# Neighbourhood attention on one core: the maxima of the next two heads taken ahead of this two's weights on VectorE

## The chip, the cores and the metric

The kernel runs on one core of one Trainium2 chip. The metric is the time of one execution on the device in microseconds (us), a median of several runs. All times below are us unless marked ns. TensorE is called PE in the profile's rows, VectorE DVE, ScalarE ACT, GpSimd POOL, SyncE SP; PEld is TensorE's weight load.

## What is computed

The whole program is two blocks of a model one after the other, with a batch of one: a first block (two layers of feed-forward, a pool/convolution/retention mixer, feed-forward) and a second block of an even layer (neighbourhood attention beside an mLSTM) and an odd layer (latent attention). The change lies in the neighbourhood attention of the even layer, over 8 heads of 64 features, 256 context tokens and 256 latent tokens (4 rows of 64). Cut to what matters:

```python
s_lat = einsum('bqhd,bkhd->bhqk', q_row, k_band) * scale + bias   # latent keys, learned bias and window
s_ctx = einsum('bqhd,bkhd->bhqk', q_row, k_c) * scale             # 256 context keys
p = softmax(concatenate([s_lat, s_ctx], axis=-1), axis=-1)
out = einsum('bhqk,bkhd->bqhd', p[..., :nl], v_band) + einsum('bhqk,bkhd->bqhd', p[..., nl:], v_c)
na_c = dense_attention(heads(naq_c), heads(nak_c), heads(nav_c))  # context tokens over context keys
```

## The kernel before

Each engine has an order of instructions written out by hand, and the engines are tied by counting semaphores alone. An engine takes its instructions in that order; `wait_ge(s, n)` stops everything behind it on its engine until semaphore `s` has reached `n`.

The attention of the even layer is cut into 16 pairs, `EVEN_PAIRS`. A pair is 128 queries of two heads (`e` is 0 or 1, the first and the second head of the pair). Pairs 0 to 7 are context queries over 256 keys; pairs 8 to 15 are latent queries over 512 keys, whose bias is added by a further product on TensorE. For each pair `p` the steps are:

- scores on TensorE (`scores(p)`): two products, for pairs 8 to 15 followed by the bias product of either head. Each head has a PSUM bank; there are four banks (2, 3, 0, 1), so that the scores of pair `p + 1` take the banks of pair `p - 1`, and wait until its weights are made (`at_exp`).
- maximum on VectorE (`top(p)`, L2599 and L2600): for each head a `tensor_reduce` of the scores into a column of the small tile `STAT`, then a `tensor_scalar` that makes the negative bias of it. Both wait for the scores (`at_scores`), and signal `at_max`.
- weights on ScalarE (`weights(p)`, L1868): `exp` of the scores into `probs[e]` (tile `PR`), with the sum of each row. It waits for `at_max`, and for the turning of pair `p - 1`, since `PR` has one buffer for each head.
- normalisation on VectorE (`norm(p)`, L2606 and L2608): reciprocal of the sum, and `PR` times it. It waits for `at_exp` and signals `at_probs`.
- turning on TensorE (`turn(p)`, L1202): transposes of `PR` into PSUM, which wait for `at_probs`; ScalarE copies them (`copy_turned`, L1878, tile `PTT`).
- values on TensorE (`values(p)`), the copy of the result by ScalarE (`place_high`, L1884) and the low part of it by VectorE (`place`, L2614).

TensorE's order around pair `p` is scores(p + 1), turn(p), values(p - 1), and then at some pairs a product of the mLSTM's head norm (`between`, `head_norm`): a mean, a variance or a spread, over 512 columns. VectorE's part of the head norm is L2581 (subtract the mean), L2585 and L2590, ScalarE's L1848, L1851, L1854 and L1858. The engines that follow wait for the last pair: `even_output` on TensorE begins with `pe.wait_ge(at_out, len(EVEN_PAIRS))`.

The same function `attend` serves the odd layer's latent attention (`base` is then 16 and not 0), with its tiles `PRO` and `PTO`.

Of the kernel before, what the change touches and what calls it, by code (L numbers as in the profile page):

```python
# [11 lines left out]
ALU = mybir.AluOpType  # L12
ACT = mybir.ActivationFunctionType
AX = mybir.AxisListType
# [57 lines left out]
def build(nc, A, out):  # L72
    with ExitStack() as ctx:
        def sem(name):
            return ctx.enter_context(nc.semaphore(name))
# [102 lines left out]
        STAT = low.put("STAT", [64])  # L178
# [86 lines left out]
        def values_of(b):  # L265

            return PS[:, 6, 0:P] if b < len(EVEN_PAIRS) else PS[:, 6 + b % 2, 0:P]
# [85 lines left out]
        def halves(name):  # L353
# [11 lines left out]
        at_scores, at_max, at_exp, at_probs, at_turned, at_copied, at_pv, at_high, at_out = (  # L365
            sem("at_scores"), sem("at_max"), sem("at_exp"), sem("at_probs"), sem("at_turned"), sem("at_copied"),
            sem("at_pv"), sem("at_high"), sem("at_out"))
# [1074 lines left out]
        def _(act):  # L1442
# [417 lines left out]
            def softmax(pairs, base, probs, turned, banks, between):  # L1860
                def weights(p):
                    w = pairs[p]["keys"]
                    for e in range(2):
                        n = 2 * (base + p) + e
                        act.wait_ge(at_max, n + 1)
                        if p >= 1:
                            act.wait_ge(at_turned, n - 1)
                        act.activation(probs[e][:, 0:w], PS[:, banks[(2 * p + e) % len(banks)], 0:w], ACT.Exp,  # L1868
                                       bias=STAT[:, 4 + e:5 + e], scale=pairs[p]["scale"],
                                       accum_out=STAT[:, 8 + e:9 + e]).then_inc(at_exp, 1)  # L1870

                def copy_turned(p):
                    nk = pairs[p]["keys"] // P
                    for e in range(2):
                        act.wait_ge(at_turned, 2 * (base + p) + e + 1)
                        if base + p >= 1:
                            act.wait_ge(at_pv, base + p)
                        act.copy(turned[e][:, 0:nk, :], PS[:, 4 + e, 0:nk * P].rearrange("p (a b) -> p a b", a=nk))\  # L1878
                            .then_inc(at_copied, 1)

                def place_high(p):
                    b = base + p
                    act.wait_ge(at_pv, b + 1)
                    act.copy(pairs[p]["out"][0], values_of(b)).then_inc(at_high, 1)  # L1884

                for p in range(len(pairs)):
                    weights(p)
                    if p >= 2 and base == 0:
                        place_high(p - 2)
                    if p >= 1:  # L1890
                        copy_turned(p - 1)
                    if p >= 2 and base:
                        place_high(p - 2)
                    between(2 * p)
                    between(2 * p + 1)
                copy_turned(len(pairs) - 1)
                place_high(len(pairs) - 2)
                place_high(len(pairs) - 1)
# [133 lines left out]
        def _(v):  # L2032
# [342 lines left out]
            vs = Steps(v, vec_step)  # L2375
# [216 lines left out]

            def attend(pairs, base, probs, banks, between):
                def top(p):
                    w = pairs[p]["keys"]
                    for e in range(2):
                        v.wait_ge(at_scores, 2 * (base + p) + e + 1)
                        src = PS[:, banks[(2 * p + e) % len(banks)], 0:w]
                        vs.link(v.tensor_reduce(STAT[:, e:e + 1], src, AX.X, ALU.max))  # L2599
                        v.tensor_scalar(STAT[:, 4 + e:5 + e], STAT[:, e:e + 1], -pairs[p]["scale"], None, ALU.mult)\  # L2600
                            .then_inc(at_max, 1)

                def norm(p):
                    for e in range(2):
                        v.wait_ge(at_exp, 2 * (base + p) + e + 1)
                        vs.link(v.reciprocal(STAT[:, 12 + e:13 + e], STAT[:, 8 + e:9 + e]))  # L2606
                        q = probs[e][:, 0:pairs[p]["keys"]]
                        v.tensor_scalar(q, q, STAT[:, 12 + e:13 + e], None, ALU.mult).then_inc(at_probs, 1)  # L2608

                def place(p):  # L2610
                    b = base + p
                    v.wait_ge(at_high, b + 1)
                    hi, lo = pairs[p]["out"]
                    v.tensor_tensor(lo, values_of(b), hi.bitcast(F32), ALU.subtract).then_inc(at_out, 1)  # L2614

                top(0)
                for p in range(len(pairs)):
                    norm(p)
                    if p >= 2 and base == 0:
                        place(p - 2)  # L2620
                    if p + 1 < len(pairs):
                        top(p + 1)
                    if p >= 2 and base:
                        place(p - 2)
                    between(2 * p)
                    between(2 * p + 1)
                for p in range(len(pairs) - 2, len(pairs)):
                    place(p)
# [110 lines left out]
            even_inputs()  # L2739
            mlstm()  # L2740
            attend(EVEN_PAIRS, 0, PR, (2, 3, 0, 1), lambda n: head_norm(n - HEAD_SHIFT))
            even_output()
            ffn_both()
            odd_inputs()
            attend(ODD_PAIRS, len(EVEN_PAIRS), PR2, (0, 1, 2, 3), lambda n: None)
            rest(O_WO + 3)
            odd_output()
# [182 lines left out]
```

## Time and profile before

| | us |
|---|---|
| median of 3 runs | 2183.38 (2182.88 to 2185.84) |
| the profiled execution | 2183.48 |
| its span in the trace | 2181.6 |
| TensorE busy in the span | 2115.5 (97%) |
| VectorE busy | 1570.3 (72%) |
| ScalarE busy | 1054.4 (48%) |

The profiled execution is within 0.1 us of the median, and 1.9 us of it lie outside of the span. The attention of the even layer runs from 1300.34, where TensorE begins the scores of pair 0, to 1374.88, where it begins the output product: 74.5 us. That of the odd layer runs from 1869.84 to some 1935. Times of single rows are from the start of the span. Where the trace gives the records of a group of matmuls, their duration reaches from the first start to the last end, which is modelled.

### The profile page before, as it was taken

Reading aid. Unit: us, or ns where it says so; the run is one execution under the profiler, and the core shown is the slowest. Engines: PE = TensorE matmul, PEld = TensorE weight load, DVE = VectorE, ACT = ScalarE, POOL = GpSimd, SP = SyncE. Lnnn points to the kernel's source line nnn. Section 1 sums busy time; section 2 is a strip of 40 time slices with the busy share of each in tenths; the row PEclk is TensorE's granted clock in tenths of the full one; section 3 lists DMA queues with packets and bytes.
Section 4 is the critical chain, followed back from the end, with each engine's and each line's share of the span. In section 5 each row is a group of like instructions: output and inputs, shape, how many; then the busy total and the mean of one; then the engine's idle time right before and its main releaser. Section 6 shows DMA issues by size and latency. Waiting matters only on the chain. (4 is left out here: it accounts for less than half of the span.)

```text
span 2181.6 us, 35138 instructions
## 1 busy us (share of the span) xinstructions
PE 2115.5 (97%) x14758; PEld 1927.2 (88%) x14758; DVE 1570.3 (72%) x2371; ACT 1054.4 (48%) x1546; POOL 156.4 (7%) x195
## 2 busy tenths in 40 slices
PE   8999999999999999999999988999999999999997
PEld 8999989999999998999897775898888887579997
DVE  6878998877988798988852667466555346858774
ACT  6443656443544465644552446345444224746652
POOL 1200102201200100200100000000000001000000
PEclk9999999999999999999999999999999999999998
DMA  7665526666566543777331120123222222023552
GB/s 272 234 232 203 206 97 251 234 241 250 208 233 245 206 155 116 272 273 257 125 120 54 59 97 13 55 78 115 97 97 97 97 89 82 24 78 118 191 175 97
DMA packets 48334, 334.93 MB, mean 154 GB/s; under 512 B 5612, under 2 KB 6716, under 8 KB 8880
## 3 DMA queue, kind: packets, MB, share of 16 engines
q1 hardware_dynamic: 38384, 267.47, 34.6%
q0 software_dynamic: 9792, 65.21, 7.8%
q8 instruction: 117, 1.92, 0.4%
q14 instruction: 41, 0.34, 0.0%
HBM read 331.61 MB, written 1.05 MB: 152 GB/s over the span
## 5 line engine op out<-in xcount | busy, mean ns | idle before, releaser
L2042 DVE TENSOR_TENSOR WLO<-RAW,WHI 128x2048 fp32r<-128x2048 f32 x252 | 574.7, 2285 | 217.9 <-ACT WHI L1457 215.2
L464 PE MATMUL PS<-XB,WHI 128*128 128x256 f32 (+1 forms) x3072 | 697.4, 322 | 8.3 <-DVE XB L2398 4.0
L1457 ACT CAST WHI<-RAW 128x2048 fp32r<-128x2048 f32 x252 | 476.6, 1894 | 281.0 <-DMA RAW<-in_dn_c 78.4
L464 PEld LDWEIGHTS PS<-XB,WHI 128*128 128x128 f32 x3072 | 513.9, 191 | 55.7 <-issue 11.0
L464 PE MATMUL PS<-XHI,WHI 128*128 128x272 f32 (+1 forms) x1760 | 498.4, 290 | 5.8 <-ACT XHI L1465 5.8
L464 PE MATMUL PS<-XB,WLO 128*128 128x256 f32 (+1 forms) x1536 | 492.1, 320 | 0.0
L464 PE MATMUL PS<-XHI,WLO 128*128 128x272 f32 (+1 forms) x1760 | 489.7, 288 | 0.0
L464 PE MATMUL PS<-XLO,WHI 128*128 128x272 f32 (+1 forms) x1760 | 482.1, 287 | 2.3 <-DVE XLO L2088 2.3
L464 PEld LDWEIGHTS PS<-XHI,WHI 128*128 128x128 f32 x1760 | 328.8, 189 | 9.8 <-issue 8.8
L464 PEld LDWEIGHTS PS<-XLO,WHI 128*128 128x128 f32 x1760 | 323.0, 189 | 4.1 <-DVE XLO L2088 3.6
L464 PEld LDWEIGHTS PS<-XHI,WLO 128*128 128x128 f32 x1760 | 326.0, 188 | 0.0
L464 PEld LDWEIGHTS PS<-XB,WLO 128*128 128x128 f32 x1536 | 292.8, 191 | 21.3
L464 PE MATMUL PS<-GHI,WHI 128*128 128x272 f32 (+1 forms) x704 | 200.1, 286 | 0.0
L464 PE MATMUL PS<-GHI,WLO 128*128 128x272 f32 (+1 forms) x704 | 199.7, 285 | 0.0
L464 PE MATMUL PS<-GLO,WHI 128*128 128x272 f32 (+1 forms) x672 | 191.9, 286 | 0.0
L2442 DVE SCALAR_TENSOR_TENSOR AC<-CB,FCW,AC 128x512 f32<-128x512 f32 (+1 forms) x176 | 97.1, 614 | 131.6 <-ACT AC L1715 103.8
L464 PEld LDWEIGHTS PS<-GHI,WLO 128*128 128x128 f32 x704 | 132.5, 188 | 0.0
L464 PEld LDWEIGHTS PS<-GHI,WHI 128*128 128x128 f32 x704 | 132.4, 188 | 0.0
L1517 ACT ACTIVATE SG<-PS 128x272 f32<-128x272 f32 (+1 forms) x88 | 34.5, 393 | 201.1 <-PE PS L464 200.7
L2071 DVE CUSTOM_DVE_ANT_0 PROD<-AW,SCB,ADAB 128x1024 f32<-128x1024 f32 x96 | 130.9, 1364 | 0.3 <-ACT SCB L1445 0.3
L2071 DVE CUSTOM_DVE_ANT_0 AW<-AW,SCB,ADAB 128x1024 f32<-128x1024 f32 x96 | 127.0, 1323 | 0.0
L464 PEld LDWEIGHTS PS<-GLO,WHI 128*128 128x128 f32 x672 | 126.4, 188 | 0.0
(364 smaller groups left out, 2517.0 us busy)
## 6 DMA issues: line engine op xcount, KB each, us to landing
AW<-in_ada POOLq DMA_DIRECT2D x48, 1024.0 KB, 7.1
RAW<-in_up_c SPq DMA_DIRECT2D x44, 1024.0 KB, 4.9
RAW<-in_up_a SPq DMA_DIRECT2D x42, 1024.0 KB, 5.2
RAW<-in_up_b SPq DMA_DIRECT2D x42, 1024.0 KB, 4.9
RAW<-in_mix SPq DMA_DIRECT2D x30, 1024.0 KB, 4.9
RAW<-in_dn_a SPq DMA_DIRECT2D x22, 1024.0 KB, 4.9
RAW<-in_dn_b SPq DMA_DIRECT2D x22, 1024.0 KB, 5.0
RAW<-in_dn_c SPq DMA_DIRECT2D x22, 1024.0 KB, 5.0
```

The costliest lines, as they stand in the source:

```text
L464: return pe.matmul(o, w, x, start=first, stop=last)
L1457: act.copy(WHI1[:, s, 0:w], RAW[:, s, 0:w]).then_inc(w1_high, 1)
L1517: act.activation(SG[r, f % 2, tk], PS[r, 2 * (f % 3), tk], ACT.Silu).then_inc(silu1_done, 1)
L2042: v.tensor_tensor(WLO1[:, s, 0:w], RAW[:, s, 0:w], WHI1[:, s, 0:w].bitcast(F32), ALU.subtract)\
L2071: v.tensor_tensor_reduce(PROD[:, :] if g == 0 else w, w, SCB[:, g, :], 1.0, ADAB[:, t:t + 1], ALU.mult, ALU.add, MODF[:, t, g:g + 1]).then ...
L2442: return v.scalar_tensor_tensor(o, i, vec(a, t), o, ALU.mult, ALU.add)
```

## The change

In `attend`, VectorE takes `top(p + 1)` ahead of `norm(p)` for the even layer, where it took it behind `norm(p)` and `place(p - 2)`. For the odd layer (`base` not 0) the order stays. As the maxima of pair `p + 1` are now written while the sums of pair `p` are still to be used, the columns of `STAT` come in two sets, 16 columns apart, chosen by `p % 2`, on VectorE and on ScalarE, in both layers.

```diff
@@ ScalarE, weights(p)
                         act.activation(probs[e][:, 0:w], PS[:, banks[(2 * p + e) % len(banks)], 0:w], ACT.Exp,
-                                       bias=STAT[:, 4 + e:5 + e], scale=pairs[p]["scale"],
-                                       accum_out=STAT[:, 8 + e:9 + e]).then_inc(at_exp, 1)
+                                       bias=STAT[:, 16 * (p % 2) + 4 + e:16 * (p % 2) + 5 + e], scale=pairs[p]["scale"],
+                                       accum_out=STAT[:, 16 * (p % 2) + 8 + e:16 * (p % 2) + 9 + e]).then_inc(at_exp, 1)
@@ VectorE, attend
                 def top(p):
-                    w = pairs[p]["keys"]
+                    w, c = pairs[p]["keys"], 16 * (p % 2)
...
-                        vs.link(v.tensor_reduce(STAT[:, e:e + 1], src, AX.X, ALU.max))
+                        vs.link(v.tensor_reduce(STAT[:, c + e:c + e + 1], src, AX.X, ALU.max))
...
                 def norm(p):
                     for e in range(2):
                         v.wait_ge(at_exp, 2 * (base + p) + e + 1)
-                        vs.link(v.reciprocal(STAT[:, 12 + e:13 + e], STAT[:, 8 + e:9 + e]))
+                        c = 16 * (p % 2) + e
+                        vs.link(v.reciprocal(STAT[:, c + 12:c + 13], STAT[:, c + 8:c + 9]))
...
                 top(0)
                 for p in range(len(pairs)):
+                    if p + 1 < len(pairs) and base == 0:
+                        top(p + 1)
                     norm(p)
                     if p >= 2 and base == 0:
                         place(p - 2)
-                    if p + 1 < len(pairs):
+                    if p + 1 < len(pairs) and base:
                         top(p + 1)
```

How VectorE's instructions stand in a row where the latent queries are worked on. PR_138 and PR_139 are the weights of the first and second head of the pair; the words in brackets are the semaphores. Before, between the placing of pair 6 and that of pair 7:

```order
L2606 RECIPROCAL STAT<-STAT 128x1 [waits at_exp]
L2608 TENSOR_SCALAR PR_138<-PR_138,STAT 128x512 [waits vec_step]
L2606 RECIPROCAL STAT<-STAT 128x1 [waits at_exp]
L2608 TENSOR_SCALAR PR_139<-PR_139,STAT 128x512 [waits vec_step]
L2614 TENSOR_TENSOR XB<-PS,XB 128x128 [waits at_high]
L2599 TENSOR_REDUCE STAT<-PS 128x1 [waits at_scores]
L2600 TENSOR_SCALAR STAT<-STAT 128x1 [waits vec_step]
L2599 TENSOR_REDUCE STAT<-PS 128x1 [waits at_scores]
L2600 TENSOR_SCALAR STAT<-STAT 128x1 [waits vec_step]
```

With the change:

```order
L2599 TENSOR_REDUCE STAT<-PS 128x1 [waits at_scores]
L2600 TENSOR_SCALAR STAT<-STAT 128x1 [waits vec_step]
L2599 TENSOR_REDUCE STAT<-PS 128x1 [waits at_scores]
L2600 TENSOR_SCALAR STAT<-STAT 128x1 [waits vec_step]
L2607 RECIPROCAL STAT<-STAT 128x1 [waits at_exp]
L2609 TENSOR_SCALAR PR_138<-PR_138,STAT 128x512 [waits vec_step]
L2607 RECIPROCAL STAT<-STAT 128x1 [waits at_exp]
L2609 TENSOR_SCALAR PR_139<-PR_139,STAT 128x512 [waits vec_step]
L2615 TENSOR_TENSOR XB<-PS,XB 128x128 [waits at_high]
```

The two maxima of the next pair, with their wait for its scores, now stand ahead of the normalisation of this pair and of the placing. The lines of the functions below `top` are one higher in the changed kernel.

TensorE's row is the same in both kernels. For the latent queries, from the scores of pair `p + 1` on (G and BIAS are operands of the scores and the bias, IDN of the turning, PTT of the values):

```order
L464 MATMUL PS<-G 128x512 [waits at_exp,at_max]
L464 MATMUL PS<-G 128x512
L464 MATMUL PS<-BIAS_146,IDN_115 128x256 [waits tab_loaded]
L464 MATMUL PS<-BIAS_146,IDN_115 128x256
L1202 MATMUL PS<-IDN,PR_138 128x128 [waits at_copied,at_probs]
L1202 MATMUL PS<-IDN,PR_138 128x128 x3
L1202 MATMUL PS<-IDN,PR_139 128x128 [waits at_copied,at_probs]
L1202 MATMUL PS<-IDN,PR_139 128x128 x3
L464 MATMUL PS<-PTT_140,VN 64x128 [waits at_out,at_copied]
```

Nothing moved here: the turning of pair `p` (L1202) stands directly behind the scores and the bias of pair `p + 1`.

## Rows read from the trace of the kernel before

**Rows 1.** The page's first part: busy time of each engine

```profile
PE 2115.5 (97%) x14758; PEld 1927.2 (88%) x14758; DVE 1570.3 (72%) x2371; ACT 1054.4 (48%) x1546; POOL 156.4 (7%) x195
```

**Rows 2.** Stretches: length, busy time (instructions) of each engine, PE clock, DMA

```profile
1300.34:1326.50 26.16, 20.35 (x121) 9.86 (x120) 18.83 (x70) 13.74 (x49) 2.65 (x5) 0.93 0.28 101
1326.50:1369.00 42.50, 36.98 (x256) 22.79 (x255) 29.86 (x85) 28.66 (x72) 0.00 (x0) 0.98 0.08 26
1869.80:1935.00 65.20, 61.63 (x449) 39.28 (x449) 50.91 (x145) 44.96 (x114) 0.04 (x1) 1.00 0.03 12
```

**Rows 3.** Waits, 1300.3 to 1374.9: waiter, waited for, total, times, longest

```profile
ACT PR L1868 <- DVE STAT L2600: 9.1, 9, 2.6
PE PS L1202 <- DVE PR L2608: 7.6, 6, 2.8
...
PE PS L1202 <- ACT PTT L1878: 3.6, 3, 2.1
```

**Rows 4.** Timeline at pair 14, 512 keys: start, duration, instructions [idle before]

```profile
1362.71 0.69 DVE L2599 TENSOR_REDUCE STAT<-PS 128x1 f32<-128x512 f32 x1 [1.05 <-PE PS L464]
...
1362.94 1.04 PE L1202 MATMUL PS<-IDN,PR 128*128 128x128 f32 x8
...
1364.29 0.74 DVE L2585 SCALAR_TENSOR_TENSOR G<-G,MLG,PS 128x512 f32<-128x512 f32 x1
```

**Rows 5.** Timeline, VectorE: one normalisation over 512 keys

```profile
1336.21 0.16 DVE L2606 RECIPROCAL STAT<-STAT 128x1 f32<-128x1 f32 x1 [2.28 <-ACT PR L1868]
...
1336.41 0.49 DVE L2608 TENSOR_SCALAR PR<-PR,STAT 128x512 f32<-128x512 f32 x1
```

**Rows 6.** Timeline at pair 6, 256 keys

```profile
1324.30 0.65 PE L1202 MATMUL PS<-IDN,PR 128*128 128x128 f32 x4
...
1324.40 0.42 DVE L2599 TENSOR_REDUCE STAT<-PS 128x1 f32<-128x256 f32 x1 [0.18 <-PE PS L464]
...
1325.45 0.68 DVE L2581 TENSOR_TENSOR G<-G,PS 128x512 f32<-128x512 f32 x1
```

**Rows 7.** Timeline at pair 2: normalisation, and the turning that waits for it

```profile
1310.13 0.35 DVE L2608 TENSOR_SCALAR PR<-PR,STAT 128x256 f32<-128x256 f32 x1
...
1310.54 0.90 PE L1202 MATMUL PS<-IDN,PR 128*128 128x128 f32 x4 [0.58 <-DVE PR L2608]
```

**Rows 8.** Timeline: the turnings of pairs 0, 4, 7, 9, 12 and 15

```profile
1303.01 0.90 PE L1202 MATMUL PS<-IDN,PR 128*128 128x128 f32 x4 [1.53 <-DVE PR L2608]
...
1317.62 0.68 PE L1202 MATMUL PS<-IDN,PR 128*128 128x128 f32 x4 [2.10 <-ACT PTT L1878]
...
1328.27 0.68 PE L1202 MATMUL PS<-IDN,PR 128*128 128x128 f32 x4 [0.61 <-ACT PTT L1878]
...
1337.63 1.12 PE L1202 MATMUL PS<-IDN,PR 128*128 128x128 f32 x8 [1.40 <-DVE PR L2608]
...
1352.72 1.11 PE L1202 MATMUL PS<-IDN,PR 128*128 128x128 f32 x8 [0.69 <-DVE PR L2608]
...
1367.81 1.94 PE L1202 MATMUL PS<-IDN,PR 128*128 128x128 f32 x8 [2.81 <-DVE PR L2608]
```

**Rows 9.** TensorE in short stretches: length, busy, clock, DMA share, GB/s

```profile
1306.00:1309.00 3.00, 3.00 (x12) 0.50 0.56 232
...
1317.60:1321.00 3.40, 2.96 (x18) 1.00 0.02 5
...
1367.80:1371.30 3.50, 3.47 (x24) 0.58 0.00 0
```

**Rows 10.** Timeline: values and head mean at either clock

```profile
1306.18 1.12 PE L464 MATMUL PS<-PTT,VN 128*64 128x128 f32 x8
...
1307.23 2.08 PE L464 MATMUL PS<-G,ONES 128*128 128x512 f32 x2
...
1311.37 0.66 PE L464 MATMUL PS<-PTT,VN 128*64 128x128 f32 x8
...
1311.96 1.13 PE L464 MATMUL PS<-G,ONES 128*128 128x512 f32 x2
```

More of the change, by code:

```diff
@@ L2598, in top @@
                         src = PS[:, banks[(2 * p + e) % len(banks)], 0:w]
-                        vs.link(v.tensor_reduce(STAT[:, e:e + 1], src, AX.X, ALU.max))
-                        v.tensor_scalar(STAT[:, 4 + e:5 + e], STAT[:, e:e + 1], -pairs[p]["scale"], None, ALU.mult)\
+                        vs.link(v.tensor_reduce(STAT[:, c + e:c + e + 1], src, AX.X, ALU.max))
+                        v.tensor_scalar(STAT[:, c + 4 + e:c + 5 + e], STAT[:, c + e:c + e + 1], -pairs[p]["scale"], None, ALU.mult)\
                             .then_inc(at_max, 1)
@@ L2605, in norm @@
                         v.wait_ge(at_exp, 2 * (base + p) + e + 1)
-                        vs.link(v.reciprocal(STAT[:, 12 + e:13 + e], STAT[:, 8 + e:9 + e]))
+                        c = 16 * (p % 2) + e
+                        vs.link(v.reciprocal(STAT[:, c + 12:c + 13], STAT[:, c + 8:c + 9]))
                         q = probs[e][:, 0:pairs[p]["keys"]]
-                        v.tensor_scalar(q, q, STAT[:, 12 + e:13 + e], None, ALU.mult).then_inc(at_probs, 1)
+                        v.tensor_scalar(q, q, STAT[:, c + 12:c + 13], None, ALU.mult).then_inc(at_probs, 1)
                 def place(p):
```

## The prediction

> **What bounds the kernel now.** The page comes first: TensorE is busy for 97% of the span [rows 1], so what stops TensorE costs the whole, and what stops another engine costs nothing until TensorE waits for it. Next the stretches: the reader is to see that the even layer's attention is a place where TensorE does stop. It is busy for 20.35 of 26.16 us over the pairs of 256 keys and for 36.98 of 42.50 us over those of 512, while VectorE has 18.83 and 29.86 us of work; the odd layer's attention, whose order stays, is busy for 61.63 of 65.20 [rows 2]. Behind the stage TensorE goes on to the output product only when the last pair is placed, so a microsecond won or lost here goes through to the end: in the rest of the program nothing waits for a clock time, only for the step ahead of it.
>
> Third, the waits of the stage. TensorE waits at the turnings (L1202) alone in any quantity: 7.6 us for VectorE's normalised weights and 3.6 us for ScalarE's copies, 11.2 us in nine waits [rows 3]. ScalarE's weights wait 9.1 us for the maxima. That is what an earlier maximum could shorten. But the last column of it is an engine that is not the bound.
>
> Last, the timeline at one pair, for which condition ends last. At pair 14 the first maximum of pair 15 starts at 1362.71, and VectorE had been idle for 1.05 us before it, waiting for TensorE's bias product. The turning of pair 14 starts at 1362.94, directly behind that product and with no wait in its row [rows 4]: its weights had been normalised while TensorE was still at the scores of pair 15. The same stands at pair 6: turning at 1324.30, first maximum of pair 7 at 1324.40, for which VectorE again waited [rows 6]. So the maxima of pair p + 1 are taken as soon as the scores exist, and at the moment when they exist the turning of pair p starts on TensorE. There is nothing to gain in such a pair by taking them ahead of the normalisation; and the normalisation that was hidden under the scores would now stand behind them.
>
> **The change part by part.** No instruction is added or removed. The second set of columns changes addresses only; the operations keep their shapes, so I take 0 for it, in both layers. The odd layer keeps its order: 0. The even layer has fifteen places (p = 0 to 14) at which two maxima with their wait for the scores go ahead of two normalisations. What is queued behind the waiting maximum is norm(p), and behind it place(p - 2) and VectorE's head norm; for norm(p) waits turn(p), for that TensorE with everything that follows, and ScalarE's weights of pair p + 1, which need the turned `PR`.
>
> *Over 512 keys, pairs 8 to 14.* The first maximum cannot start before 1362.71 in the case of the rows, since the scores decide it. Behind the two maxima and their `tensor_scalar`s VectorE takes its next instruction at 1364.29 [rows 4]. That is now the reciprocal, if the weights are ready (they are: for pair 14 they were made some microseconds before). The multiplication starts 0.20 behind the reciprocal (1336.21, 1336.41) and lasts 0.49 [rows 5]; from the end of one to the turning are 0.06 (1310.13 + 0.35 to 1310.54) [rows 7]. So the turning starts at 1364.29 + 0.20 + 0.49 + 0.06 = 1365.04 and not at 1362.94: a wait of 2.10 us for each pair, seven times, 14.7 us.
>
> *Pair 7.* Maxima over 512 keys, normalisation over 256 (0.35): 1.96 us.
>
> *Over 256 keys, pairs 1 to 6.* The same with rows 6: 1325.45 + 0.20 + 0.35 + 0.06 = 1326.06 and not 1324.30: 1.76 us, six times, 10.6 us.
>
> *Pair 0.* The scores of pair 1 are there already; two maxima go between the weights and the reciprocal. A pair of them over 256 keys takes 1325.45 - 1324.40 = 1.05 us, of which a part falls where VectorE is waiting for the first weights anyway: between 0 and 1.05 I take 0.8 us.
>
> *The second head.* A turning that waits for its normalisation waits again for the second head's: it then lasts 0.90 where an undelayed one lasts 0.65 over 256 keys, and 1.12 where it lasts 1.04 over 512 [rows 4, 7, 8]. Three of the eight pairs of 256 have it now (pairs 0 and 2 are in the rows) and pairs 9 and 12 of those of 512. That leaves 0.25 more at five pairs of 256 and 0.08 at five of 512: 1.6 us.
>
> *What goes.* The waits that TensorE has now at the turnings of pairs 1 to 14 are not added to the new ones: each turning waits for what comes last. They are the 11.2 us less the first (1.53) and the last (2.81) of them [rows 3, 8]: 6.9 us. The longest, 2.10 at pair 4, was for ScalarE's copies, which were late because ScalarE's order had it wait for the head norm on VectorE; the new waits are as long and cover it.
>
> *The end.* Pair 15 has no next pair. Its wait of 2.81 us stays in kind; VectorE's L2585, which now starts 1.35 us behind the turning of pair 14 (1364.29 against 1362.94) and holds up ScalarE's last weights, would stand behind one normalisation and a placing instead, about 0.7 us behind it: 0.7 less.
>
> Sum: 14.7 + 2.0 + 10.6 + 0.8 + 1.6 - 6.9 - 0.7 = 22.1 us. I take 22; the places where my counting is doubtful (the overlap at pair 0, waits of the scores' own that shrink) take rather than give, by perhaps 1. On the profiled execution's 2183.5 us, which is the median of the runs within 0.1, that gives 2205.
>
> *TensorE's clock.* Twice in the stage TensorE is on the lower of its levels (1.2 GHz): the rows show a granted clock of 0.50 from 1306 to 1309 and 0.58 over 1367.8 to 1371.3 [rows 9]. The first came behind the wait of 1.53 us at pair 0 and a second shorter one, the last behind the wait of 2.81 us at pair 15; the 2.10 us at pair 4 were followed by a full clock, 1.00 over 1317.6 to 1321 [rows 8, 9]. A low stretch costs 1.12 - 0.66 for values and 2.08 - 1.13 for a head mean, 1.4 us [rows 10]. My sum leaves both where they are. The bounds: none of the two remains, 2.8 less; or more of them come, each 1.4 more. With 15 waits of about 2 us in place of nine mostly short ones, more is likelier than fewer. The page "TensorE: Matmul & The Clock Gate" of the Trainium skill, in its section "A second HAM failure mode: psum-queue depth-cycling", says that short idle pieces between groups of matmuls can make the clock go to and fro between its two levels, and that this costs throughput. It speaks against this change; the row at pair 4 does not bear it out, the one at pair 0 does. By the rule the low level would be met at many of the new waits; by the row at pair 4 at hardly any.
>
> **The rivals.**
> - *The clock follows the waits.* If every second of the sixteen waits brings a low stretch, there are 8 in place of 2: 6 x 1.4 = 8.4 us more, 2213. For it: two of the nine waits now, and that the pairs of 256 keys have the least work between waits. Against it: pair 4, and pairs 9 and 12. A chance of 0.15.
> - *The early pairs lose nothing.* TensorE is idle for 5.8 of the 26.16 us over 256 keys [rows 2]. If the new waits there only took the place of those, the 512 half would stay: 14.7 + 2.0 + 0.4, less the 2.7 us of waits that it has now (0.61, 1.40 and 0.69 at pairs 7, 9 and 12 [rows 8]) and the 0.7 of the end: 13.7, so 2197. Against it: at pair 6 the turning waits for nothing [rows 6], and the scores end later than the weights there. 0.06.
> - *Faster.* ScalarE's weights wait 9.1 us for maxima [rows 3]; if the maxima came earlier and the normalisation were not held up, TensorE's 6.9 us between pairs 1 and 14 could go: 2176.5. The point from which it decides is whether the scores of pair p + 1 are complete before the weights of pair p are. At pair 14 they would have to be 2.1 us earlier, and at pair 6 1.8. TensorE's order puts them behind turning, values and head norm of the pairs before, and that does not change. 0.03.
> - *No effect.* The order would have to be indifferent, VectorE never reaching the maximum before its scores are there. VectorE waited 1.05 and 0.18 us for them even in the old place [rows 4, 6]. 0.02.
>
> **How the numbers follow.** The forecast, 2205, has 0.74. Its own range is 2201 to 2209: one or two low stretches fewer, up to three more, 1 or 2 us in the counting. The range for all is 2198 to 2214, which takes in most of the rival of the clock and the lower end of doubtful counting. About 0.2%, 4.4 us, is what can be told from no change here. Faster by more than that: 0.02; within: 0.02; slower: 0.96.
>
> **What would show it.** In the changed kernel's trace the stage from the first scores to the output product lasts 96 to 97 us in place of 74.5. TensorE's wait at L1202 for the normalised weights appears at almost every pair, some 2.1 us over 512 keys and 1.8 over 256, some 30 us in all in place of 7.6; the wait for ScalarE's copies shrinks to pair 15. VectorE's reciprocal waits no more for ScalarE except at the last pair, and its maxima wait for TensorE instead. ScalarE's weights wait for the turning and not for the maxima. Everything outside of the stage, the odd layer included, keeps its length within a microsecond. The prediction is wrong if turnings start directly behind the scores of the next pair, if the granted clock is low over long parts of the stage, or if another stage gives time back.

## The result, and the profile after

| | before | after |
|---|---|---|
| median of the runs, us | 2184.57 | 2217.78 |
| profiled execution's span, us | 2181.6 | 2216.4 |
| mean granted clock of the span | 0.994 | 0.985 |
| the even layer's attention, us | 74.5 | 108.6 |

The change makes the kernel slower: the ratio is 1.015, with an interval of 1.0138 to 1.0162, or 33 us. I had forecast 22 us, and a range that ended at 2214. The amount of low clock is much the same in each of the four executions, whose mean granted clocks are 0.984 to 0.986. The ratios below leave out one execution, of e11, which took 3000.82 us at a mean granted clock of 0.65.

First the stretches of the changed kernel: length, busy time and number of instructions of TensorE, weight load, VectorE, ScalarE and GpSimd, then the granted clock, the DMA share and GB/s. The first is the stage over pairs of 256 keys, the second over those of 512 with the end, then the whole stage, what lies ahead of it, what lies behind it, and the odd layer's attention.

```profile
1300.52:1340.87 40.35, 27.95 (x118) 13.04 (x117) 18.54 (x70) 14.31 (x51) 2.65 (x5) 0.62 0.19 66
1340.87:1409.16 68.29, 49.49 (x294) 27.90 (x293) 30.28 (x87) 30.23 (x76) 0.00 (x0) 0.87 0.05 16
1300.52:1409.16 108.64, 77.44 (x409) 40.95 (x409) 48.82 (x157) 44.55 (x125) 2.65 (x5) 0.78 0.10 35
0.00:1300.50 1300.50, 1276.61 (x9520) 1212.73 (x9520) 1037.32 (x1509) 626.03 (x865) 140.42 (x181) 1.00 0.54 193
1409.16:2216.00 806.84, 779.34 (x4830) 680.97 (x4830) 483.58 (x705) 383.95 (x557) 13.32 (x9) 0.99 0.29 100
1904.00:1970.00 66.00, 61.58 (x448) 39.24 (x448) 52.15 (x144) 45.81 (x114) 0.00 (x0) 1.00 0.05 17
```

The same stage before:

```profile
1300.34:1374.87 74.53, 60.71 (x409) 35.24 (x408) 49.27 (x157) 44.28 (x125) 2.65 (x5) 0.95 0.14 50
```

The stage starts at the same time within 0.2 us and is 34.1 us longer, of the 34.8 us by which the span grew; behind it there is no repayment. TensorE did the same 409 recorded instructions. Its idle time went from 74.5 - 60.7 = 13.8 to 108.6 - 77.4 = 31.2 us, which is 17.4 more, and its busy time from 60.7 to 77.4, which is 16.7 more. That is not yet the split between waiting and clock, since the record of a turning also covers its wait for the second head (at the full clock 1.25 us over 512 keys here, 1.04 before [rows 4]); e10 below parts the two. That the clock has a share is in its column: 0.78 over the stage in place of 0.95. If the clock has but the two levels 1.00 and 0.50, a mean of 0.78 over 108.6 us is 2 x 0.22 x 108.6 = 48 us at the lower level (1.2 GHz), and before 2 x 0.05 x 74.5 = 7.5 us.

The waits of the stage, as in [rows 3]: who waited for whom, us in total, times, longest.

```profile
DVE STAT L2599 <- PE PS L464: 37.9, 14, 5.2
ACT PR L1868 <- PE PS L1202: 31.2, 11, 4.6
PE PS L1202 <- DVE PR L2609: 28.6, 16, 2.3
...
ACT PR L1868 <- DVE STAT L2600: 2.6, 1, 2.6
```

The change does what it says. ScalarE's weights wait for the maxima once, at the first pair, and not for 9.1 us. But they now wait 31.2 us for the turnings; the maxima wait 37.9 us for TensorE's scores; and all sixteen turnings wait for VectorE. The timeline at the turning of pair 11, with the scores and the maxima of pair 12 ahead of it, shows the loop, and answers to [rows 4]:

```profile
1373.45 1.13 PE L464 MATMUL PS<-BIAS,IDN 128*128 128x256 f32 x4
1374.19 0.69 DVE L2599 TENSOR_REDUCE STAT<-PS 128x1 f32<-128x512 f32 x1 [3.71 <-PE PS L464]
...
1375.77 0.15 DVE L2607 RECIPROCAL STAT<-STAT 128x1 f32<-128x1 f32 x1
1375.96 0.49 DVE L2609 TENSOR_SCALAR PR<-PR,STAT 128x512 f32<-128x512 f32 x1
...
1376.50 1.25 PE L1202 MATMUL PS<-IDN,PR 128*128 128x128 f32 x8 [1.92 <-DVE PR L2609]
```

VectorE had stood for 3.71 us in front of a maximum whose scores did not exist, with the reciprocal that TensorE needed behind it. From the first maximum to the turning are 2.31 us; I had worked out 2.33 (1362.71 to 1365.04). The full clock held here. Where it did not, TensorE alone in short stretches (length, busy, clock, DMA share, GB/s):

```profile
1303.00:1313.00 10.00, 7.38 (x26) 0.52 0.60 227
1318.00:1321.00 3.00, 1.30 (x10) 0.92 0.00 0
1321.00:1344.00 23.00, 17.96 (x67) 0.50 0.00 1
1360.00:1398.00 38.00, 26.62 (x172) 1.00 0.09 29
```

For 23 us on end the clock is at its lower level, and for 38 us on end at its upper. The waits at the turnings are the shorter ones in the first, 1.68 us at each of its three turnings over 256 keys, and 1.92 at the six over 512 keys in the second:

```profile
1331.70 1.15 PE L1202 MATMUL PS<-IDN,PR 128*128 128x128 f32 x4 [1.68 <-DVE PR L2609]
```

### The profile page after: what moved, and what is told of

It is laid out like the page before. It is cut to its first block and busy times, and to the rows that moved or that the text cites. A ratio compares the mean times of both kernels' runs of the same rounds, so it can differ in the third digit from the quotient of the medians.

```text
span 2216.4 us, 35138 instructions
## 1 busy us (share of the span) xinstructions
PE 2133.4 (96%) x14758; PEld 1934.6 (87%) x14758; DVE 1569.7 (71%) x2371; ACT 1054.5 (48%) x1546; POOL 156.4 (7%) x195
## 3 DMA queue, kind: packets, MB, share of 16 engines
q8 instruction: 117, 1.92, 0.3%
HBM read 331.61 MB, written 1.05 MB: 150 GB/s over the span
```

## The experiments

All ratios are to runs of the kernel before on the same chip. "A product of constants" is a matmul of tiles of ones into a PSUM bank that nobody reads then; it changes no result. `keep_busy(n, bank)` issues n of them.

**e1: the columns alone.** The order of before with the two sets of columns:

```diff
-                    if p + 1 < len(pairs) and base == 0:
+                    if p + 1 < len(pairs) and base == 0 and False:
                         top(p + 1)
```

> The order of before with the two sets of columns alone. Theory (the order costs the time): no difference that can be measured, within 2 us of before. Rival (the second set of columns costs something, on VectorE or ScalarE): slower by a part of the 33 us of the change, and then in the odd layer's attention too, which is 1.0 us longer or more in the trace.

0.9995 (0.9985 to 1.0004), and the stage is that of before:

```profile
1299.46:1374.01 74.55, 60.91 (x409) 35.36 (x408) 49.27 (x157) 44.20 (x125) 2.65 (x5) 0.95 0.14 50
```

The second set costs nothing that can be measured, 2 us either way. What is left is the order.

**e2 and e3: each half of the change.** The maxima ahead for `p < 7` alone, and for `p >= 7` alone:

```diff
-                    if p + 1 < len(pairs) and base == 0:
+                    if p + 1 < len(pairs) and base == 0 and p < 7:      # e3: p >= 7
                         top(p + 1)
                     norm(p)
...
-                    if p + 1 < len(pairs) and base:
+                    if p + 1 < len(pairs) and (base or not (p < 7)):    # e3: p >= 7
                         top(p + 1)
```

> The maxima go ahead only for p = 0 to 6, whose next pair has 256 keys. Theory (waits of 1.7 us at the turnings, and a low clock because TensorE works for too small a share of the time there): the waits alone give 10.6 + 0.8 + 1.2 - 4.2 = 8.4 us, the clock some 8 to 12 us more, so 16 to 20 us slower than before, with the granted clock about 0.6 up to the end of pair 6. Rival (waits only, the clock fell by chance): 8 to 9 us slower. Second rival (the clock falls because of the longer waits over 512 keys): 8 to 9 us too, with a clock near 0.93 over the first eight pairs.

> The maxima go ahead only for p = 7 to 14, whose next pair has 512 keys. Theory: the waits give 14.7 + 2.0 + 0.4 - 2.7 - 0.7 = 13.7 us; from pair 9 on the clock was full in the changed kernel in spite of waits of 2.1 us, so the clock adds 0 to 3 us: 13 to 17 us slower than before. Rival (each wait of 2 us brings the clock down): 20 us or more slower, with a low clock in the stretches of pairs 8 to 14.

e2: 1.0052 (1.0035 to 1.0068), some 11 us. e3: 1.0089 (1.0073 to 1.0105), some 20 us. The two stretches by keys and the stage, for e2:

```profile
1300.32:1339.15 38.83, 26.38 (x118) 11.78 (x117) 18.54 (x70) 14.29 (x51) 2.65 (x5) 0.70 0.19 68
1339.15:1387.57 48.42, 41.56 (x294) 25.32 (x292) 30.53 (x87) 29.93 (x76) 0.00 (x0) 0.96 0.07 23
1300.32:1387.57 87.25, 67.94 (x409) 37.11 (x408) 49.07 (x157) 44.22 (x125) 2.65 (x5) 0.84 0.12 43
```

and for e3:

```profile
1325.97:1397.22 71.25, 52.51 (x294) 30.52 (x292) 30.93 (x89) 31.13 (x77) 0.00 (x0) 0.83 0.04 15
1299.98:1397.22 97.24, 73.14 (x409) 40.63 (x408) 49.17 (x157) 44.53 (x125) 2.65 (x5) 0.84 0.11 38
```

Both halves lose, and 11 + 20 is nearly the whole 33. Both are off my expectation, in opposite ways: less in the context half (16 to 20 expected), more in the latent half (13 to 17 expected, and its rival had 20 or more). I had placed the low clock by the trace of the changed kernel, which has it low in the first 40 us; with the latent half of the change alone it is low in the latent half, 0.83, for 2 x 0.17 x 71.25 = 24 us. So the trace of one execution of one kernel did not say where the clock would fall.

**e4: the waits filled.** The changed kernel with products of constants ahead of each turning:

```diff
                         n = 2 * (base + p) + e
-                        pe.wait_ge(at_probs, n + 1)
                         if n >= 2:
                             pe.wait_ge(at_copied, n - 1)
+                        if base == 0 and e == 0:
+                            keep_busy(6 if p < 7 else 8 if p < 15 else 5, 4)
+                        pe.wait_ge(at_probs, n + 1)
```

> The changed kernel, with products of constants into a bank that is free at that moment ahead of each turning of the even layer's attention (6 for p below 7, 8 for p = 7 to 14, 5 for p = 15), so that TensorE works during the waits instead of idling. They are extra work and change no result. Theory (22 us of waits that stay, and 12 us of low clock that goes): 2204 to 2209, 11 us or so under the changed kernel, with the granted clock above 0.95 over the stage. Rival (the waits alone are 33 us long, the clock matters little): no faster than the changed kernel, 2215 or more.

1.0151 (1.0132 to 1.0169), as slow as the changed kernel, which looks like the rival. It is not, by its trace: the clock is 1.00 over the whole stage, but the filling outlasts the waits. First six products (two records each) ahead of a turning, then the stage:

```profile
1310.06 2.86 PE L464 MATMUL PS<-ONES 128*128 128x256 f32 x12 [0.58 <-ACT PTT L1880]
```

```profile
1304.48:1413.36 108.88, 104.46 (x631) 76.05 (x630) 48.72 (x157) 44.08 (x125) 2.65 (x5) 1.00 0.10 35
```

A product takes 0.45 us, and I had taken it for half of that. The run tells nothing between the theories.

**e5 and e10: a shorter filling, and a single product.** As e4, with `3 if p < 7 else 4 if p < 15 else 3`, and with `1 if p < 15 else 0`.

> The changed kernel with fewer products of constants ahead of each turning: 3 for p below 7 and for p = 15, 4 for p = 7 to 14. In the run before this one each such product took 0.45 us, so that 6 of them (2.86 us) outlasted the wait of 1.7 us that they were to fill, and the clock was 1.00 throughout; 3 take 1.4 us and 4 take 1.85, less than the waits of 1.7 and 2.1. They are extra work and change no result. Theory (about 20 us of waits stay, and 12 us of low clock go): 2203 to 2209, and a granted clock of 0.97 or more over the stage. Rival (the low clock costs nothing beyond the waits): 2215 or more.

> The changed kernel with one product of constants (0.45 us) ahead of each turning of pairs 0 to 14, extra work that changes no result. It leaves about 1.3 us of idle time in each wait over 256 keys and 1.65 over 512. Two theories of what the clock follows. Theory (idle time on TensorE: the less, the less often the clock falls): a good part of the 13.5 us that three or four products gave back comes already, 2206 to 2212. Rival (only an unbroken row of work holds the clock, a third of the wait filled does nothing): 2216 to 2219.

e5: 1.0088 (1.0072 to 1.0103), 2204.29 us. e10: 1.0092 (1.0077 to 1.0107), 2206.29 us beside 2186.89 of before. The stage in e5, and in e10 with the 12 us behind it:

```profile
1300.98:1396.76 95.78, 86.28 (x521) 53.76 (x520) 48.73 (x157) 44.19 (x125) 2.65 (x5) 1.00 0.11 39
```

```profile
1300.79:1394.86 94.07, 69.15 (x439) 38.11 (x438) 48.73 (x157) 44.33 (x125) 2.65 (x5) 1.00 0.11 40
1394.86:1406.86 12.00, 12.00 (x100) 12.00 (x101) 5.37 (x4) 4.02 (x4) 0.15 (x2) 1.00 0.00 1
```

This is the run that parts the two causes. Extra work on the engine that bounds the kernel made the changed kernel faster, by 1.015 - 1.0092, which is 13 us. In e10 the product lies inside the wait and delays nothing; the turning still waits for VectorE, as here at pair 12:

```profile
1367.84 0.69 DVE L2601 TENSOR_REDUCE STAT<-PS 128x1 f32<-128x512 f32 x1 [2.67 <-PE PS L464]
1368.07 0.59 PE L464 MATMUL PS<-ONES 128*128 128x256 f32 x2
...
1370.15 1.31 PE L1204 MATMUL PS<-IDN,PR 128*128 128x128 f32 x8 [1.49 <-DVE PR L2611]
```

Again 2.31 us from first maximum to turning. So e10 has the change's waits at their full length and none of the low clock, and its stage lasts 94.1 us: against 74.5 of before less the 2.8 us that I had put on the two low stretches there, an estimate, the waits cost 22.4 us. About 1 us of that is the experiment's own: from the turning of pair 10 to that of pair 11, both at the full clock, are 7.43 us in e10 (1356.35 to 1363.78) and 7.36 in the changed kernel (1369.14 to 1376.50), and that fifteen times. The rest, 108.6 - 94.1 = 14.6 us, is the clock, some 0.30 us for each of the 48 us at the lower level. Less the 2.8 us that before had of it, 11.8 us of the 34.1 by which the stage grew are the clock's.

**e11 and e12: the filling in one half.** As e5, with `3 if p < 7 else 0`, and with `0 if p < 7 else 4 if p < 15 else 3`.

> The changed kernel with three products of constants ahead of the turnings of pairs 0 to 6 alone. In the changed kernel's trace the low clock stands mostly there (0.62 on the mean over the first 40 us of the stage against 0.87 over the rest). Theory (the low clock belongs to the place): most of the 13.5 us comes back here, 8 to 10, so 2208 to 2210, and the latent pairs keep their 0.87. Rival (where the clock falls is not bound to the place, and the run with early maxima in the latent half alone had it low there): the latent pairs show a lower clock than 0.87, and the gain is 3 to 7 us, 2211 to 2215.

> The changed kernel with four products ahead of the turnings of pairs 7 to 14 and three at pair 15 alone. Theory (the low clock belongs to the place): 3 to 5 us come back, 2213 to 2215, with the clock over the first 40 us of the stage near 0.62. Rival (not bound to the place): 6 to 9 us come back, 2209 to 2212, as the runs with half of the change had 2.8 us over their waits in the context half and 6.8 in the latent half.

e11: 1.0137 (1.0117 to 1.0157). e12: 1.0131 (1.0116 to 1.0146). The halves of e11, then of e12:

```profile
1303.03:1335.09 32.06, 28.54 (x160) 16.53 (x159) 18.43 (x70) 13.51 (x49) 2.65 (x5) 1.00 0.23 82
1335.09:1408.56 73.47, 54.22 (x294) 31.50 (x292) 30.30 (x87) 30.88 (x77) 0.00 (x0) 0.81 0.05 15
```

```profile
1299.63:1338.37 38.74, 25.61 (x117) 11.58 (x117) 18.56 (x70) 13.55 (x49) 2.65 (x5) 0.74 0.19 68
1338.37:1405.54 67.17, 61.39 (x364) 39.80 (x362) 30.36 (x87) 30.67 (x77) 0.00 (x0) 0.93 0.05 16
```

e11 gives back 3 us, with an uncertainty of some 5, where the theory that the low clock belongs to the context half wanted 8 to 10. e12 comes to 1.9 thousandths below the changed kernel, 4 us, with an uncertainty of some 4: that is what the theory of the place gave it (3 to 5), under the 6 to 9 of the rival, and it excludes neither. The clocks do not decide it either. The unfilled latent half of e11 shows 0.81 where the changed kernel has 0.87, but e3, with the same order there, has 0.83; and the unfilled context half stood at 0.62 in the changed kernel, 0.70 in e2 and 0.74 in e12. Each is the trace of one execution, so shifts of this size come without a filling, and it is not shown that filling one half lowers the clock in the other. (The unfilled turnings of e11 and e12 also have the order of semaphore waits of e4; they wait 2.01 and 1.77 us where the changed kernel's wait 1.92 and 1.68.) What is shown is that the filled half keeps its clock: 1.00 in e11's context half, and in e12 what is low of the latent half lies at its beginning and behind the turning of pair 14.

**e6: the scores earlier.** TensorE takes the scores of the pair after next directly behind a turning:

```diff
                 scores(0)
+                if base == 0:
+                    scores(1)
                 for p in range(len(pairs)):
-                    if p + 1 < len(pairs):
+                    if p + 1 < len(pairs) and base:
                         scores(p + 1)
                     turn(p)
+                    if p + 2 < len(pairs) and base == 0:
+                        scores(p + 2)
                     if p >= 1:
                         values(p - 1)
```

> The changed kernel, and TensorE takes the scores of pair p + 2 directly behind the turning of pair p, ahead of the values and the head norm's product, so that the maxima of a pair are taken while TensorE has other work. Theory (what costs is that the maximum stands behind scores that come directly before the turning): the waits at the turnings shrink where values and a head norm's product now lie between, from 2.1 to some 0.5 to 1.5 us, but not in the first pairs; 8 us less waiting than the changed kernel, and less low clock, so 2200 to 2210. Rival (early maxima cost by VectorE's own work, wherever the scores stand): 2215 or more. Second rival (with the scores early the early maxima pay, as ScalarE's weights no longer wait): under the time of before.

1.0086 (1.0072 to 1.0099), 2204.34 us.

```profile
1299.06:1393.24 94.18, 69.81 (x409) 38.12 (x408) 48.64 (x157) 44.78 (x125) 2.65 (x5) 0.87 0.11 40
```

```profile
PE PS L1202 <- DVE PR L2613: 18.9, 10, 3.0
...
PE PS L1202 <- ACT PTT L1882: 2.9, 2, 1.6
```

With work between the scores and the turning, the waits at the turnings fall from 28.6 us in 16 to 21.8 in 12, and the time at the lower level from 48 to 2 x 0.13 x 94.2 = 24 us. The price of an early maximum depends on where the scores stand, as the theory has it. It does not turn into a gain. The longest waits that are left, 3.01 us, come where VectorE's order has a step of the head norm (L2589) ahead of the maxima, and that step waits for TensorE's product, as here ahead of the turning of pair 13:

```profile
1371.93 0.75 DVE L2589 SCALAR_TENSOR_TENSOR G<-G,MLG,PS 128x512 f32<-128x512 f32 x1 [4.15 <-PE PS L464]
1374.90 1.55 PE L1202 MATMUL PS<-IDN,PR 128*128 128x128 f32 x8 [3.01 <-DVE PR L2613]
```

An early maximum with that step behind it was not tried, so whether the order can be made to pay is open.

**e8: the square of the head norm later.** On the kernel before, not on the changed one:

```diff
-                if n - 2 in MEAN_AT:
-                    h = MEAN_AT.index(n - 2)
+                if n - 3 in MEAN_AT:
+                    h = MEAN_AT.index(n - 3)
                     act.wait_ge(head_step, HEAD_CENTRED[h])
```

> The kernel before, and ScalarE takes the square of the head norm one half step later in its order (at n - 3 in place of n - 2), so that the weights and copies of pairs 4 and 7 do not stand behind a square that waits for VectorE. Theory (the wait of 2.10 us at the turning of pair 4, and 0.61 at pair 7, come from ScalarE's order): 1.5 to 3 us under before, 2181 to 2183. Rival (the wait only moves to the next turning): no difference.

0.9985 (0.9977 to 0.9994). The stage is 2.6 us shorter, and the turning of pair 4 waits 0.53 in place of 2.10 us [rows 8]:

```profile
1302.95:1374.86 71.91, 60.52 (x409) 35.40 (x408) 49.18 (x157) 44.42 (x125) 2.75 (x5) 0.94 0.15 52
1374.86:1386.86 12.00, 12.00 (x83) 12.00 (x84) 5.37 (x4) 3.82 (x3) 0.15 (x2) 0.80 0.01 2
```

```profile
1318.58 0.84 PE L1202 MATMUL PS<-IDN,PR 128*128 128x128 f32 x4 [0.53 <-DVE PR L2608]
```

In this execution some of it is given back at once: in the 12 us behind the stage the clock is 0.80. It is the longest of the eleven, 2185.34 us against a median of 2183.05 (and 2185.20 of before), so it need not be typical there.

**e9 and e13: the square later, and the clock held up.** e9 adds three products at pair 0 and five at pair 15, placed as in e4. e13 has one at pair 0 and four at pair 15 and places them ahead of every wait, the last ones in a bank of scores that is free:

```diff
+                        if base == 0 and e == 0 and p in (0, 15):
+                            keep_busy(1 if p == 0 else 3, 4 if p == 0 else 2)
                         pe.wait_ge(at_probs, n + 1)
...
                     it, b = pairs[p], base + p
+                    if base == 0 and p == 15:
+                        keep_busy(1, 2)
                     pe.wait_ge(at_copied, 2 * b + 2)
```

> The kernel before with the later square, and with 3 products of constants ahead of the turning of pair 0 and 5 ahead of that of pair 15, where TensorE waits for 1.53 and 2.81 us and the clock then falls. Theory (each low stretch costs 1.4 us and goes when TensorE works through the wait): 4 to 6 us under before, with no stretch of the stage at a low clock: 2178 to 2181. Rival (the clock falls by the pairs of 256 keys as such, which leave TensorE idle for a fifth of the time): only the gain of the square.

> The kernel before with the later square, and single products of constants (0.45 us each, extra work that changes no result) where TensorE waits longest: one ahead of the turning of pair 0, three ahead of that of pair 15 and one ahead of its values, the last four into a bank of scores that is free by then and so without a wait for ScalarE's copies. Theory (one product in a wait is enough to keep the clock up, and in the earlier try the products at pair 15 stood behind the wait for the copies and came too late): no stretch at a low clock from the first scores to 12 us behind the stage, 2.6 us by the square and 3 to 4 by the clock, 5 to 7 us under before, 2178 to 2181. Rival (the end of the stage leaves TensorE idle for too long whatever is put into it): a low clock behind pair 15 and 2 to 3 us under before, as with the square alone.

e9: 0.9993 (0.9984 to 1.0002), nothing won that can be measured. At pair 0 its three products did hold the clock, where it was 0.50 from 1306 to 1309 before [rows 9]:

```profile
1304.00:1308.00 4.00, 3.15 (x21) 1.00 0.98 410
1308.00:1312.00 4.00, 3.25 (x20) 1.00 0.20 71
```

Its five products at pair 15 stood behind the wait for ScalarE's copies, so TensorE idled for 2.73 us first, the clock fell and they took 3.88 us:

```profile
1364.63 3.88 PE L464 MATMUL PS<-ONES 128*128 128x256 f32 x10 [2.73 <-ACT PTT L1880]
```

e13: 0.9969 (0.9957 to 0.9982), 6.8 us faster than before and the fastest kernel here. The traces place 3.3 us of it in the stage (74.53 to 71.28); where the rest arises is not shown. Its stage, the 12 us behind it, a stretch behind pair 0, and the end:

```profile
1299.70:1370.98 71.28, 63.04 (x420) 36.42 (x419) 49.30 (x157) 44.48 (x125) 2.66 (x5) 0.95 0.14 52
1370.98:1382.98 12.00, 12.00 (x100) 12.00 (x101) 5.37 (x4) 4.02 (x4) 0.15 (x2) 1.00 0.00 1
1306.00:1309.00 3.00, 3.00 (x12) 1.17 (x12) 0.04 (x2) 1.45 (x7) 0.46 (x1) 0.50 0.33 134
1364.00:1368.00 4.00, 2.76 (x26) 1.99 (x26) 1.92 (x5) 2.10 (x7) 0.00 (x0) 1.00 0.00 0
```

At the end and behind it the clock stays full; behind pair 0, where one product had been put into the wait, it falls as before. So the expectation of no low stretch at all was wrong, and the mechanism that it rests on, one product is enough, holds in e10 and not here. What differs behind pair 0 is that e10 has a product in the wait of pair 1 too, and that e9 has three at pair 0.

## Why the prediction was wrong

*The maximum blocks the normalisation.* Right. Every turning waits for VectorE, nearly every early maximum for scores (14 waits in the row above); e1 excludes the columns. *The price of a wait.* Right: 2.31 us from first maximum to turning where I had 2.33, 28.6 us of waits at the turnings where I had some 30, and e10, where nothing but the waits is left of the change, gives 22.4 us where the sum had 22.1. That these two are so near is in part luck: the term of the second head was too small, as a turning over 512 keys lasts 0.21 us longer (1.25 against 1.04) where I had 0.08, and 22.4 rests on the estimate of 2.8 and has the experiment's own 1 us in it. *What goes and what stays outside.* Right: the odd layer's attention keeps its 61.6 us of TensorE, and 34.1 of 34.8 us arose inside the stage.

*TensorE's clock.* This is the step that failed: "My sum leaves both where they are. The bounds: none of the two remains, 2.8 less; or more of them come, each 1.4 more", and the forecast that allowed for "up to three more". The sum thus put the clock's added cost at nothing, though the same passage called more stretches likelier than fewer. The time at the lower level went from 7.5 to 48 us, and those 48 us cost 14.6 us, 11.8 more than the 2.8 that I had on before. The direction was in the text, and so was the rival that brought it about, "every second of the sixteen waits brings a low stretch". My use of it was wrong in two ways. I gave it 0.15, on the strength of one wait of 2.10 us that had been followed by a full clock; and I sized it as separate stretches of some 3.4 us, when the low level lasted for 23 us on end, over three turnings. Its time, 2213, was 5 us short of the result. The rule of the Trainium skill that I had set against the row ("TensorE: Matmul & The Clock Gate", "A second HAM failure mode: psum-queue depth-cycling") was the better guide: short idle pieces between groups of matmuls, and a clock that goes to and fro. The trace agrees with it, with 0.78 over the stage, and e5 and e10 show the throughput coming back when the pieces are filled, in e10 with idle pieces of 1.05 and 1.49 us left. It leaves open the 38 us of full clock with waits of 1.92 us.

*The rivals on the other sides.* The chance of a faster kernel stands as 0.03 at its rival and as 0.02 in the last line, a slip that changes nothing. "The early pairs lose nothing" falls with e2, 11 us over those pairs alone. "Faster" needed the scores before the weights; e6 goes part of that way and is still 19 us slower than before.

What stays open is what brings the clock down at one wait and not at the next of the same length. The full clock from 1360 to 1398, behind waits of 1.92 us, and the low one from 1321 to 1344, behind waits of 1.68, exclude the length of the wait alone; the latent half at 0.87, 0.83 and 0.81 and the context half at 0.62, 0.70 and 0.74 under the same order exclude that the place alone fixes it. Which of the many waits decides, and how many products it takes behind pair 0 (one in e13 is too few, three in e9 are enough, as is one there and one at pair 1 in e10), these runs don't settle.

## What to carry to other kernels

Before an operation is put earlier on an in-order engine, look up when its input exists, and what then stands behind it: here the input came directly ahead of the consumer of the work that was pushed back, so that all of that work became a wait of the bounding engine. When new waits of a microsecond or two are strung over a stage of short matmuls, price them twice, once as idle time and once as the same matmuls at the lower clock, and take the second as likely unless rows show many such waits with a full clock. A cheap test of how much is clock is one dummy product inside each wait, issued before the engine stands at any long semaphore wait (in e9 it came behind one, and the clock had fallen).

## What the runs showed that I had not expected

One product of 0.45 us in each wait of some 2 us, fifteen in all, kept the granted clock at 1.00 over 94 us, where it was 0.78 without them, and made the kernel 13 us faster; four products did no better. In e8 and in the changed kernel the clock stayed low behind the stage too, where TensorE was busy without a break: 0.80 and 0.86 over 12 us, against 1.00 in e13. The kernel before has 1.00 there as well, with the waits at its end (2.81 and 1.82 us) that e8 has. So a wait at the end of a stage can be paid for in the next one, and need not be. First before, then the changed kernel:

```profile
1374.87:1386.87 12.00, 11.99 (x100) 11.99 (x101) 5.37 (x4) 4.01 (x4) 0.15 (x2) 1.00 0.01 2
1409.16:1421.16 12.00, 12.00 (x87) 12.00 (x88) 5.37 (x4) 3.82 (x3) 0.15 (x2) 0.86 0.01 2
```
